# One YOCO decoder step on one core: eight sample sequences packed two to a pair, their join spread over the last two head pairs, key products interleaved with transposes, first weight slab loaded in halves

## The reference

```python
s_past = q_lat . c_past + q_rope . kr_past        # (8 sequences, 16 heads, 1024 keys)
s_new  = q_lat . c_new  + q_rope . kr_new
p = softmax(concat(s_past, s_new) * ATTN_SCALE)
o_lat = p[:P] . c_past + p[P:] . c_new
o = einsum('blhc,chv->blhv', o_lat, w_uv);  h = h + o @ w_o
```

## Time and profile before

| | us |
|---|---|
| median of 3 runs | 806.02 (803.4 to 806.13) |
| profiled execution, its own time | 807.03 |
| its span in the profile | 805.3 |
| mean granted TensorE clock | 0.975 of full |
| pairs 0 to 7 up to the output projection | 439.5 to 551.6 |

### The profile page before, as it was taken

How to read it: one execution, slowest core, us unless ns; L and a number is a source line. 1 busy time by engine, 2 the same in 40 slices (tenths; PEclk the granted TensorE clock), 3 DMA queues, 4 the chain that set the end, 5 groups by cost and what they waited for, 6 DMA issues and landing times.

```text
span 805.3 us, 17011 instructions
## 1 busy us (share of the span) xinstructions
PE 761.8 (95%) x6391; PEld 740.5 (92%) x6391; DVE 337.7 (42%) x771; ACT 402.7 (50%) x688; POOL 548.2 (68%) x254
## 2 busy tenths in 40 slices
PE   4899899999999999999989999978999999999994
PEld 3899899999999999999888787768999999999993
DVE  5697655424232322224886555541224323231104
ACT  6567454546444444555664555522456444444441
POOL 7576665987878888986875212212878888888880
PEclk9999999999999999999999999976999999999997
DMA  8354343555766655555474888601454555555631
GB/s 304 107 181 157 131 142 125 194 184 187 257 235 232 226 183 183 201 192 183 154 282 149 245 263 257 242 27 53 162 191 161 193 183 182 182 176 193 205 133 54
DMA packets 45352, 146.75 MB, mean 182 GB/s; under 512 B 5651, under 2 KB 6931, under 8 KB 45043
## 3 DMA queue, kind: packets, MB, share of 16 engines
q1 hardware_dynamic: 45154, 145.62, 53.9%
q0 software_dynamic: 144, 0.40, 0.1%
HBM read 144.52 MB, written 1.48 MB: 181 GB/s over the span
## 4 chain that ended last, share of the span: by engine, by line
PE 44%; DVE 4%; ACT 2%; issue 1%; DVEq 0%; ACTq 0%
PE ps L1186 14%; PE ps L1187 13%; PE ps L1188 13%; ACT tt L678 1%; PE ps L1515 1%; PE ps L1482 1%; PE ps L1404 0%; PE ps L1528 0%; DVE work L773 0%; DVE tt L1082 0%; DVE h L1178 0%; PE ps L1428 0%; DVE olo L752 0%; PE ps L1472 0%; DVE krzlo L752 0%
## 5 line engine op out<-in xcount | busy, mean ns | idle before, releaser
L384 POOL TENSOR_TENSOR wlo<-raw,whi 128x1024 fp32r<-128x1024 f32 x227 | 541.0, 2400 | 236.8 <-ACT whi L448 236.6
L1186 PE MATMUL ps<-xhi,whi 128*128 128x264 f32 x1080 | 314.0, 291 | 15.5 <-DVE xlo L797 11.7
L1187 PE MATMUL ps<-xlo,whi 128*128 128x264 f32 x1080 | 308.9, 286 | 0.0
L1188 PE MATMUL ps<-xhi,wlo 128*128 128x264 f32 x1080 | 308.5, 286 | 0.0
L448 ACT ACTIVATE whi<-raw 128x1024 fp32r<-128x1024 f32 x227 | 238.9, 1054 | 57.9 <-PE ps L1188 53.9
L1186 PEld LDWEIGHTS ps<-xhi,whi 128*128 128x128 f32 x1080 | 206.3, 191 | 17.4 <-issue 8.4
L1187 PEld LDWEIGHTS ps<-xlo,whi 128*128 128x128 f32 x1080 | 206.8, 191 | 0.2
L1188 PEld LDWEIGHTS ps<-xhi,wlo 128*128 128x128 f32 x1080 | 205.5, 190 | 0.0
L1186 PE MATMUL ps<-ahi,whi 128*128 128x264 f32 x352 | 100.0, 284 | 0.0
L1188 PE MATMUL ps<-ahi,wlo 128*128 128x264 f32 x352 | 99.9, 284 | 0.0
L1187 PE MATMUL ps<-alo,whi 128*128 128x264 f32 x352 | 99.9, 284 | 0.0
(11 more groups left out here) (232 smaller groups left out, 1152.1 us busy)
## 6 DMA issues: line engine op xcount, KB each, us to landing
raw<-w_stream SPq DMA_DIRECT2D x227, 512.0 KB, 3.2
pg<-pages SPq DMA_DIRECT2D x64, 288.0 KB, 3.4
pg<-w_ukT SPq DMA_DIRECT2D x1, 2048.0 KB, 8.1
pg<-w_uv SPq DMA_DIRECT2D x1, 2048.0 KB, 8.1
h<-xT SPq DMA_DIRECT2D x4, 264.0 KB, 4.6
y_out<-h SPq DMA_DIRECT2D x4, 264.0 KB, 2.1
wsraw<-wsT SPq DMA_DIRECT2D x1, 512.0 KB, 7.4
bsb<-bs SPq DMA_DIRECT2D x1, 512.0 KB, 7.7
```

The costliest lines, as they stand in the source:

```text
L384: pool.tensor_tensor(wlo[:, c % RING, :], raw[:, c % RING, :], whi[:, c % RING, :].bitcast(F32), ALU.subtract).then_inc(lo_ready, 1)
L1186: pe.matmul(out, whi_, mhi, start=start, stop=False)
L1187: pe.matmul(out, whi_, mlo, start=False, stop=False)
L1188: return pe.matmul(out, wlo_, mhi, start=False, stop=stop)
```

## The change

`MID` and `END` say which sequence runs in which pair. Pairs 0 to 5 have a sequence in the middle (0, 2, 3, 5, 6, 7). Pairs 0 and 2 also have one at the end (1 and 4), whose scores come behind `sample_attend` and whose transposes and attend come inside the next pair. Pairs 6 and 7 have none. `totals` moves to the end of pair 5 with VectorE's first half of the join (`differences`); the exponential, the second half (`weights`), `turn_weights`, `spread` and `sample_latents` move into pair 6, `sample_heads` and the transposes behind it into pair 7. `turn` and `keys` of the next pair alternate by head e. The output projection waits for the low parts of each head pair only as it comes to them. The loads of slabs PR_S+7 and PR_S+8 move behind the pages of sequences 4 and 5.

At the start the gains are loaded first and slab 0 in halves with the first activations between; ScalarE and GpSimd split it in halves. VectorE puts `h` times the gain into a PSUM bank, ScalarE copies that to `xhi`, VectorE subtracts from it to get `xlo`. TensorE makes the low-weight passes of the first four blocks after their high ones. The squares are taken behind all of this.

```diff
+        MID = (0, 2, 3, 5, 6, 7, None, None)
+        END = (1, None, 4, None, None, None, None, None)
+        JOIN = 5
...
-            load(0)
             sp.dma_start(gn[:].rearrange("p g k o -> p (g k o)"), gains).then_inc(gains_in, 16)
+            sp.dma_start(raw[:, 0, 0:SLAB // 2], w_stream[0][:, 0:SLAB // 2]).then_inc(raw_first, 16)
             sp.dma_start(h[:, 0:2, :], xk[:, 0:2, :]).then_inc(h_in[0], 16)
+            sp.dma_start(raw[:, 0, SLAB // 2:SLAB], w_stream[0][:, SLAB // 2:SLAB]).then_inc(raw_ready[0], 16)
...
+            load(PR_S + 6)
             for s in range(3, NS):
-                load(PR_S + s + 3)
                 sp.wait_ge(spv_done, s - 2)
                 load_pages(s)
-            load(PR_S + NS + 3)
+                if s in (4, 5):
+                    load(PR_S + 3 + s)
...
```

On ScalarE, at the start:

```diff
+            def first_high(m):
+                act.wait_ge(xg_done, m + 1)
+                act.activation(xhi[:, m, :], ps[:, XB[m % 3], 0:T], ACT.Copy).then_inc(xhi_done, 1)
...
```

On VectorE, at the start:

```diff
+            def first_low(m):
+                dve.wait_ge(xhi_done, m + 1)
+                lo_of(xlo[:, m, :], ps[:, XB[m % 3], 0:T], xhi[:, m, :]).then_inc(xlo_done, 1)
             for m in range(KD):
                 if m % 2 == 0:
                     dve.wait_ge(h_in[m // 2], 16)
-                prepare("mix0", m)
+                if m > 2:
+                    dve.wait_ge(xlo_done, m - 2)
+                dve.tensor_scalar(ps[:, XB[m % 3], 0:T], h[:, m, :], gn[:, G["mix0"], m, :], None,
+                                  ALU.mult).then_inc(xg_done, 1)
+                if m:
+                    first_low(m - 1)
+            first_low(KD - 1)
+            for m in range(KD):
+                add_square(NQ["mix0"], m)
...
```

On ScalarE, in the loop over pairs:

```diff
+                if p and END[p - 1] is not None:
+                    sample_turned(END[p - 1])
+                if p == JOIN + 1:
+                    act.wait_ge(dd_done, 2)
+                    act.activation(ww, dd, ACT.Exp).then_inc(ww_done, 1)
                 exponentials(p, 0)
                 values_high(p)
                 exponentials(p, 1)
+                if p and END[p - 1] is not None:
+                    sample_out(END[p - 1])
+                if MID[p] is not None:
+                    sample_exponentials(MID[p])
...
```

On VectorE, in the loop over pairs:

```diff
+                maximum(p, 0)
+                if p == JOIN + 1:
+                    weights()
+                maximum(p, 1)
...
```

On TensorE, in the loop over pairs:

```diff
                 scores(p)
+                if p and END[p - 1] is not None:
+                    turn_probs(END[p - 1])
+                values(p)
+                if p and END[p - 1] is not None:
+                    sample_attend(END[p - 1])
+                if MID[p] is not None:
+                    sample_scores(MID[p])
+                if p == JOIN + 1:
+                    turn_weights()
                 if p == PAIRS - 1:
+                    sample_heads()
+                for e in range(2):
+                    turn(p, e)
+                    if p < PAIRS - 1:
+                        keys(p + 1, e)
+                if MID[p] is not None:
+                    turn_probs(MID[p])
+                if p == JOIN + 1:
+                    sample_latents()
+                if p == PAIRS - 1:
+                    turn_sample_heads()
+                attend(p)
+                if MID[p] is not None:
+                    sample_attend(MID[p])
+                if END[p] is not None:
+                    sample_scores(END[p])
+                if p == JOIN:
+                    totals()
-            sample_latents()
-            sample_heads()
-            pe.wait_ge(olo_done, PAIRS)
             pe.wait_ge(olos_done, 1)
-            out_product("wo", 2, KS, lambda b: (ohi[:, b, :], olo[:, b, :]), None)
+            out_product("wo", 2, KS, lambda b: (ohi[:, b, :], olo[:, b, :]), lambda b: pe.wait_ge(olo_done, b // 2 + 1))
```

More of the change, by code:

```diff
@@ L1119, in weights @@
                 dve.tensor_tensor(dd[:, 4, :], mn, nsn, ALU.subtract).then_inc(dd_done, 1)
+            def weights():
                 dve.wait_ge(ww_done, 1)
@@ L1148, in _ @@
                 normal(p, 1)
[L1149 to L1154, removed]
+                if MID[p] is not None:
+                    sample_maximum(MID[p])
+                if p == JOIN + 1:
+                    spread()
+                turned_low(p, 0)
+                turned_low(p, 1)
                 if p < PAIRS - 1:
@@ L1228, in _ @@
             pe.wait_ge(const_done, 9)
-            main(0, 0, KD, x_of, ready=x_ready("mix0"))
+            pe.wait_ge(hi_first, 1)
+            for b in range(KD // 2):
+                pe.wait_ge(xlo_done, b + 1)
+                w = slice(b * P, b * P + P)
+                pe.matmul(ps[:, 0, 0:T], whi[:, 0, w], xhi[:, b, :], start=b == 0, stop=False)
+                pe.matmul(ps[:, 0, 0:T], whi[:, 0, w], xlo[:, b, :], start=False, stop=False)
+            pe.wait_ge(lo_first, 1)
+            for b in range(KD // 2):
+                pe.matmul(ps[:, 0, 0:T], wlo[:, 0, b * P:b * P + P], xhi[:, b, :], start=False, stop=False)
+            pe.wait_ge(lo_ready, 1)
+            for b in range(KD // 2, KD):
+                pe.wait_ge(xlo_done, b + 1)
+                w = slice(b * P, b * P + P)
+                last = passes(ps[:, 0, 0:T], whi[:, 0, w], wlo[:, 0, w], *x_of(b), False, b == KD - 1)
+            last.then_inc(slab_used, 1)
             main(1, 1, KD, x_of)
@@ L1355, in _, with keys @@
                 queries(p)
-            def keys(p):
+            def keys(p, e):
                 s = (PR_S + p) % RING
@@ L1363, in keys @@
                     pe.wait_ge(klo_done, p)
-                for e in range(2):
-                    for c in range(KL):
-                        w = slice((KL * e + c) * P, (KL * e + c + 1) * P)
-                        last = passes(ps[:, 4, e * NP_:(e + 1) * NP_], whi[:, s, w], wlo[:, s, w], cThi[:, c, :],
-                                      cTlo[:, c, :], c == 0, c == KL - 1)
-                last.then_inc(k_done, 1)
+                for c in range(KL):
+                    w = slice((KL * e + c) * P, (KL * e + c + 1) * P)
+                    last = passes(ps[:, 4, e * NP_:(e + 1) * NP_], whi[:, s, w], wlo[:, s, w], cThi[:, c, :],
+                                  cTlo[:, c, :], c == 0, c == KL - 1)
+                if e:
+                    last.then_inc(k_done, 1)
             def values(p):
@@ L1397, in scores, with turn @@
                     last.then_inc(sc_done, 1)
-            def turn(p):
-                for e in range(2):
-                    pe.wait_ge(pn_done, 2 * (2 * p + e) + 2)
-                    for b in range(3):
-                        last = pe.transpose(ps[:, 2 + e, b * P:b * P + P], pr[:, e, b * P:b * P + P], ident[:])
-                    last.then_inc(pt_done, 1)
+            def turn(p, e):
+                pe.wait_ge(pn_done, 2 * (2 * p + e) + 2)
+                for b in range(3):
+                    last = pe.transpose(ps[:, 2 + e, b * P:b * P + P], pr[:, e, b * P:b * P + P], ident[:])
+                last.then_inc(pt_done, 1)
             def attend(p):
@@ L1536, in _ @@
             pe.wait_ge(ctlo_done, 1)
-            keys(0)
+            for e in range(2):
+                keys(0, e)
             sample_queries()
```

140 lines of the change are left out of this document (68 added, 72 removed).

## The result

The changed kernel takes 793.89 us (median of 4 runs, 791.95 to 795.23) where the kernel before takes 804.93 (4 runs, 803.4 to 806.13): a ratio of 0.9859, 95% interval 0.9831 to 0.9888. 790.0 was forecast, with a range of 785 to 800. The profiled execution took 794.5 us, its span 792.8.

What follows compares the result with a forecast made beforehand. TensorE, busy 95% of the span, was taken as the bound, so only idle and half-clock time could go. 3.5 + 11.2 + 2.85 = 17.6, less 1.5 allowance, 16.1 us off 807.03; by the median 790, range 785 to 800.

Steps and rivals of the forecast that it cites:

- the rival with 0.35: Tail: clock falls to half; 800 us if before the latents, 794 if late, middle 796; chance 0.35.
- 1.5 of allowance: Tail: 1.5 us taken off the gain for ten new hand-overs between engines, set at 0.05 to 0.25 us each.
- The start: Up to the root: new load and engine order gains 3.5 us, bounds 2 and 4.5; root at 19.5 to 20.2.
- The ordinary pair: Pairs with one sequence: half of `keys` before the second transpose gains 0.14 us a pair, 0.8 over six.
- Two sequences to a pair: Pairs 0 to 5: end sequences cost 1.9 us in each of P0 to P3; 8.7 us given back before pair 6.
- Pairs 6 and 7: Tail at full clock: 14.2 and 9.6 us, 23.8 together, so the output projection starts 11.2 us earlier.
- The projection at full clock: Output projection: regains half of the 5.7 us that it ran at half clock, 2.85 us.
- The join's operations: Rival in pair 6: VectorE's weights with two SBUF inputs held up 2.2 us by GpSimd; 792 us, chance 0.03.
- the tail did give: Rival that the tail gives nothing, VectorE's and ScalarE's chains waiting on each other in pair 6: 802 to 804 us, chance 0.04.
- nothing starved: Rival that page loads starve the pairs, each reload taking 6.5 us longer; kernel slower from there, chance 0.03.

Runs made afterwards that it cites:

- e1: Kernel before with the new start alone: 800.49 us (10 runs), ratio 0.994 to the kernel before.
- e7: Changed kernel with its new start order, but high and low activations made from SBUF, no product in PSUM: 798.18 us, ratio 0.9913 to the kernel before.
- e6: Changed kernel with the next pair's keys behind both turns again: 796.42 us, ratio 0.9897 to the kernel before.
- e11: e9 with ScalarE's `sample_out` of the end sequence ahead of `exponentials(p, 1)`: 785.14 us (5 runs), ratio 0.9751 to the kernel before.
- e4: Changed kernel with the 16 products of the past's latents left out of `sample_latents`: 784.76 us, ratio 0.974 to the kernel before.
- e9: Changed kernel with the samples' latents turned round: 16-wide join weights stationary, sequences' outputs moving with 256 columns: 786.32 us, ratio 0.9775 to the kernel before.
- e2: Changed kernel with the old start, so the pairs' change alone: 797.06 us (4 runs), ratio 0.9892 to the kernel before.
- e12: Changed kernel with both halves of slab 0 loaded ahead of the gains and `h`: 794.36 us, ratio 0.9862 to the kernel before.
- e5: Changed kernel with VectorE's second half of the join behind the first head's `normal` in pair 6: 797.53 us, ratio 0.9911 to the kernel before.
- e3: Changed kernel with the second group of latent products moved behind `attend(6)`: 793.76 us, ratio 0.986 to the kernel before.
- e13: e9 with the next pair's keys behind both turns: 790.7 us, ratio 0.9834 to the kernel before; single runs 787.6 to 794.4.

## Why the prediction was right, and where its sum was not

**The whole.** 790.0 forecast, 793.9 measured: direction, size and range held. The case that came true is the rival with 0.35, the clock falling in the new tail (794 if late, 800 if ahead of the latents), and the forecast's own condition, a clock of 1.00 there, did not hold. The clock fell between the two places that the rival priced and not for its reason, so that the time agrees with its 794 is in part luck. Between the two profiled executions 12.5 us were gained where 16.1 were forecast: 0.9 less at the start, 0.4 more up to pair 6, 4.3 less in pairs 6 and 7, 0.2 less in the projection, and 1.5 of allowance that was not needed and hid part of the miss.

**The start: right in kind, its size within the bounds.** 3.5 us taken, 2 and 4.5 as bounds; the root moved by 4.3 in the profiled execution, and in the ten traces with this start it is at 18.97 to 19.92, 3.4 to 4.3 us earlier; e1 gave 4.8 by its ratio, with an interval of 3.6 to 6.1. The last square ended at 17.5, not 18, so that the table load behind it ended at 18.8, not 19.4; and `h` was first used at 4.90 for 5.99 before, 1.1 us earlier where 0.7 was taken. Where the gain comes from was argued as a bound and is now shown: without the product in PSUM 4 us go (e7). By the Trainium skill (SBUF — State Buffer, "Who interferes with whom") VectorE and GpSimd lock each other out of one shared port pair, and VectorE needs it with two SBUF inputs; the traces agree, 0.42 us from PSUM beside GpSimd in the changed kernel and up to 2.6 us from SBUF in e7. One thing the sum did not look at: before, the root waited for TensorE, whose matmuls of 264 columns started 0.22 us apart up to 21.3 us and 0.12 apart behind that, though the windows show a granted clock of 1.00 all the while; in the changed kernel they start 0.12 apart from 13.7 on. By these spacings some 1.6 us of the old start (16 matmuls from 17.8 to 21.3) was this slower pace. Of the 4.3 us only 2.6 reach the pairs in the profiled execution (434.99 for 437.55 at the first projection of the pairs); the kernels of this study with the same start have that mark between 432.4 and 435.0. What differs is short stretches at half clock near 25, 82 and 406 us: in the profiled one, the clock behind the fall at 82 was at half for 6.8 us.

**The ordinary pair: the gain is zero.** The copies that feed `attend` were named as what is late next, and 0.14 us was left for the interleaving. Pair 4 takes 11.26 us (490.09 to 501.35) for 11.28 before, and e6 is no slower in these pairs.

**Two sequences to a pair: right.** Pairs 1 and 3 take 12.84 and 12.85 us (13.1 forecast, with a stand of 0.93 for 1.1), pair 2 13.33 (13.2), pair 5 12.23 (12.4). Pair 6 starts 71.5 us behind the first sample scores; with the 2.6 of the start added it is at 516.1 in old terms, 516.5 was forecast. e11, where the stand is 0.34 us shorter, shows that it hangs on the place of `sample_out` in ScalarE's queue. No wait of TensorE names a page, so the pages do not starve it.

**Pairs 6 and 7: this is the step that failed.** 14.2 and 9.6 us were forecast at full clock; they took 15.65 and 12.45. At full clock the counts are right: e4's pair 6 takes 10.12 us and its left-out products 3.9, 14.0 in all; pair 7 takes 9.46 in e4 and 9.45 in e9. Together they took 28.1 us (513.58 to 541.68), and 14.0 + 9.5 makes 23.5: the 4.6 us between are half clock, more than the whole error of this step (28.1 for 23.8), and the 1.5 us allowed for hand-overs were not needed. The prediction looked for a stand long enough to bring the clock down, and priced `sample_latents` at full clock because TensorE would be busy there. It had the warning in its own rows: latents and heads never brought the clock back before, "though the records call TensorE busy". Work that did not bring the clock back then was in this place the work that lost it. That row was one execution's: with the same tail e1's clock did come back during the heads, so "never" was too strong. In all five traces of this tail (the changed kernel twice, e2, e7, e12) the clock falls in the second group, 10.9 to 12.2 us behind the start of pair 6. With e4 and e9 the cause is shown for this place, behind a stand of 1.00 us: take the 16-column products away or make them 256 wide, and the clock stays.

**The projection at full clock: right.** From its start to the end it takes 251.1 us for 253.75 before, 2.6 for 2.85.

**The other rivals.** The join's operations did not meet GpSimd, the tail did give, nothing starved.

Open: why the clock in this tail is back after 10 us (the changed kernel twice, e7) or nearly 14 (e2, e12) and in e5 and e6 only after 20, and whether the block needs the stand ahead of it. And the stretches at half clock near 25, 82 and 406 us differ from run to run and were not studied.

## What to carry to other kernels

Check a move of small matmuls for what it does to TensorE's clock and not for its busy time only: here 4.4 us of products with 128-wide weights and 16 moving columns cost as much again, 4.6 us, in slowed work, and the same products turned round, with the narrow side stationary, cost half and nothing behind. Keep short stands of TensorE apart where they can't be removed; the interleaving was worth nothing for the wait that it covered and 3 us for the clock. At a start in which GpSimd splits weights, give VectorE one input in PSUM; it was worth 4 us here. And do not take a clock's return from one trace: the same instructions had it back at different places in different executions.

## What was not expected of the hardware

- The granted clock fell from 1.00 to 0.50 inside 4.4 us of products with 16 moving columns, behind a stand of 1.00 us, with TensorE's records busy throughout (525.6 in the changed kernel, near 524.3 in e3), and held with 2.2 us of products of 256 columns in the same place (e9).
- Another 0.6 to 0.7 us of standing in pair 6, one of 1.00 us turned to 0.20 and 1.38 (e5) or a second of 0.71 behind it (e6), brought the clock down some 7.5 us behind the pair's start instead of 11 to 12, and it was at half for 20 us instead of 10 to 14. The same two stands without the block (e13) gave 787.6 us in one run and 794.4 in another.
- The clock came back in e1 at 543.0, during products with 8-wide weights; in the kernel before it stayed at half through the same ones up to 557.3.
- Beside GpSimd's subtractions two subtractions of 264 columns with two inputs in SBUF took about 2.2 and 2.6 us (e7), and 0.5 in the gap between; with one input in PSUM each took 0.42.
